# Two inner norms of a one-layer streaming encoder: the last two units before each run 384 tokens, then 256, with the norm between, and the next stage's first two units go by token halves

## The chip, the cores and the metric

One core of one Trainium2 chip runs the kernel. The metric is the device time of one execution in microseconds (us). The traces and the profile pages are of one execution each, taken by the hardware profiler; "span" is the time from the first to the last instruction in it. PE is TensorE, DVE is VectorE, ACT is ScalarE, POOL is GpSimd, SP issues the weight loads.

## The reference

One step of a hybrid encoder layer over 640 tokens: 512 of a prompt (batch 1) and 8 x 16 of samples, width 1024. Everything is fp32 in and out.

```
x += 0.5 * gate1 * SwiGLU_1(mod1(rms(x)))            # D_FF = 2816
x += gate2 * (mixer(mod2(rms(x))) @ w_out)           # w_in: 1024 -> 3664; sparse attention | gated delta net
x += 0.5 * gate3 * SwiGLU_2(mod3(rms(x)))
y  = rms(x)                                          # final norm
rms(z)  = z * rsqrt(mean(z*z over the 1024 features) + 1e-6) * gain
mod_i(z) = z * (1 + scale_i(c)) + shift_i(c)         # c: one row for the prompt, one per sample
```

"Inner norms" are the second and the third `rms`: between the first feed-forward stage and the mixer's `w_in` projection, and between the mixer's `w_out` projection and the second feed-forward stage. A norm over the features needs the sum of squares of a token over all of x, so it can't be finished for a token before the last feature tile of the stage ahead has been added for that token.

## The kernel before, in words

x is held transposed, `x_t[128, 8, 640]`: feature tile m (0 to 7) on the partitions, tokens along the row. A *unit* is one output tile of 128 features by 640 tokens. It is summed in one of two PSUM pairs (two banks, one per 320 tokens, `HALF`). A product is done in three passes so that it keeps fp32 precision: every operand is split into a rounded part (`_hi`, fp32r, made by ACT) and the remainder (`_lo`, made by DVE by a subtraction), and PE does hi x hi, hi x lo and lo x hi. So a unit over k input tiles is k x 3 x 2 matmuls of 320 columns: 36 in the last chunk of the first feed-forward stage (k = 6), 48 in the projections (k = 8). Weights are split the same way, some units ahead: `split_hi` on ACT (L335), `split_lo` on DVE (L344), in the feed-forward stages `part_hi` and `part_lo`; four slots hold split weights, and a slot is free when its unit is done.

The order of work is written out by hand for each engine; semaphores count what is done. Each engine runs its own list in order.

The stage ahead of a norm ends with eight units, one for each feature tile m of x. After each, `add_to_x` (L540) on DVE adds gate * result into `x_t`, `act_square` (L364) squares the new tile on ACT, and `pool_square_sums` (L405) on POOL adds the squares of tiles 0 to 6 into `std`. Then, at the norm:

- `sum_squares` (L3310) on PE sums over the partitions with one-column matmuls against ones: 5 token tiles of `std`, then 5 of the last square. Each fp32 matmul shows as two pieces.
- `act_std` (L376), `norm_rstd` (L389): root on ACT and reciprocal on DVE, for a column of 5 token tiles. Between the last add and the reciprocal DVE makes the tables `amp` and `gate` (L485, L506) in the first norm.
- PE (L3328) spreads the reciprocals over all partitions: 5 matmuls of 128 columns into banks 2 and 3.
- For each feature tile m: `rstd_times` (L394) on DVE multiplies x by the spread row (from PSUM), ACT scales and shifts the 512 prompt tokens, POOL does so for the 128 sample tokens in two instructions, ACT rounds (`h_hi` or `b_hi`), DVE subtracts (`h_lo` or `b_lo`). The buffers `t1` and `h32` are double. These are `act_modulate`, `dve_modulate`, `pool_modulate` (L417, L435, L459) in the first norm and the `_modulate_halves` three in the second. Only tile 0 goes in two token halves, so that the next stage can begin sooner.
- The next stage's first two units run together, one input tile at a time as it becomes ready: `project_two` (L3415) for `w_in`, `both_units` for the second feed-forward stage. For each input tile this is 12 matmuls of 320 columns.

The third unit of a next stage needs the PSUM pair of the first, so it waits until ACT has evacuated that (L1715 after the first norm, the SiLU of L1022 after the second). In the second norm ACT loads the SiLU table after its last rounding, and the fourth unit's weights are split in the midst of the norm's work (`EARLY[3]`).

The final norm is not touched. There the last four units already run for 384 tokens (`SPLIT`) and then 256.

Of the kernel before, what the change touches and what calls it, by code (L numbers as in the profile page):

```python
# [24 lines left out]
P = 128  # L25
# [178 lines left out]
def encoder_step(nc, a):  # L204

    ctx = ExitStack()
    with ctx:
# [156 lines left out]
        def act_square(act, n, x_base, m):  # L364

            if m >= 2:
                act.wait_ge(sq_summed, 6 * (n - 1) + max(m - 2, 1))
            at = 0
            if m == KD - 1:
                act.wait_ge(r_tok, 4 * n - 1)  # L370
                act.activation(sq_of[n][:, m % 2, 0:SEQ], x_t[:, m, 0:SEQ], ACT.Square).then_inc(std_done, 1)
                at = SEQ
            act.wait_ge(x_done, x_base + m + 1)
            act.activation(sq_of[n][:, m % 2, at:TOK], x_t[:, m, at:TOK], ACT.Square).then_inc(sq_done, 1)

        def act_std(act, n):  # L376

            act.wait_ge(ss_done, KD + 2 * n)
            act.activation(ss_tok[:, 1], bank[2][:, 0:NT], ACT.Sqrt, scale=1.0 / D, bias=EPS).then_inc(std_done, 1)

        def first_half(act, n, m, out, t_ap, hi):

            act.wait_ge(r_tok, 4 * n + 1)
            act.activation(out, t_ap, ACT.Identity, scale=amp[:, n, m, 0:1],
                           bias=mod[:, 3 * n * KD + m, 0:1]).then_inc(std_done, 1)
            act.wait_ge(std_done, 4 * n + 1)
            act.activation(hi, out, ACT.Copy).then_inc(std_done, 1)

        def norm_rstd(dve, n):  # L389

            dve.wait_ge(std_done, 4 * n)
            dve.reciprocal(ss_tok[:, 0], ss_tok[:, 1]).then_inc(r_tok, 1)

        def rstd_times(dve, n, out, m, halves=False):  # L394

            if halves:
                dve.wait_ge(rstd_done, 2 * n - 1)
                dve.tensor_tensor(out[:, 0:HALF], x_t[:, m, 0:HALF], bank[2][:, P:P + HALF], ALU.mult).then_inc(r_tok, 1)
                dve.wait_ge(rstd_done, 2 * n)
            at = HALF if halves else 0  # L400
            for cols, src in ((slice(at, 3 * P), bank[2][:, P + at:]), (slice(3 * P, TOK), bank[3][:, 0:2 * P])):
                ins = dve.tensor_tensor(out[:, cols], x_t[:, m, cols], src, ALU.mult)
            ins.then_inc(t_done, 1)

        def pool_square_sums(pool, n):  # L405

            for m in range(1, KD - 1):
# [5 lines left out]
                else:  # L413
                    pool.wait_ge(sq_summed, 6 * (n - 1) + m - 1)
                    pool.tensor_tensor(std_of[n], std_of[n], sq_of[n][:, m % 2], ALU.add).then_inc(sq_summed, 1)

        def act_modulate(act):  # L417
            n = 1
            act.wait_ge(tables_done, tables_at(n) + 2)
            for m in range(KD):  # L420
                g = n * KD + m
                if m == 0:
                    first_half(act, n, m, h32[:, g % 2, 0:HALF], t1[:, g % 2, 0:HALF], h_hi[:, m, 0:HALF])
                at = 0 if m else HALF
                act.wait_ge(t_done, g + 1)
                if m >= 2:
                    act.wait_ge(h_lo_done, T_LO + g - 1)
                    act.wait_ge(h_hi_done, T_HI + g - 1)
                act.activation(h32[:, g % 2, at:SEQ], t1[:, g % 2, at:SEQ], ACT.Identity,
                               scale=amp[:, n, m, 0:1], bias=mod[:, 3 * n * KD + m, 0:1]).then_inc(hp_done, 1)  # L430
                act.wait_ge(hp_done, g + 1)
                act.wait_ge(hs_done, g + 1)
                act.activation(h_hi[:, m, at:TOK], h32[:, g % 2, at:TOK], ACT.Copy).then_inc(h_hi_done, 1)
# [3048 lines left out]
```

## Time and profile before

| | us |
|---|---|
| runs (3), median | 1461.63 (1461.09 to 1462.32) |
| the profiled execution | 1461.94 |
| its span | 1460.2 |
| PE busy | 1408.6 (96%) |
| DVE busy | 897.9 (61%) |
| ACT busy | 566.6 (39%) |
| POOL busy | 387.4 (27%) |

An engine's busy time is the union of its instructions. Matmul ends are modelled, and a matmul's bar (0.31 us for 320 columns) is longer than the distance to the next one; the distance between starts is the rate. An idle engine costs nothing unless the chain that sets the end runs through it.

### The profile page before, as it was taken

To read this page: it belongs to the slowest core of one execution; us is meant where nothing else is said; L and a number is where in the kernel's file an instruction comes from. 1 tells how busy PE (TensorE), PEld (TensorE's weight loads), DVE (VectorE), ACT (ScalarE), POOL (GpSimd) and SP (SyncE) were. 2 spreads that over 40 slices of the span, in tenths; PEclk is the share of its full clock that TensorE was granted. 3 is DMA by queue.
4 is the path that set the end of the run, shared out by engine and by line. 5 is a ranking of instruction groups with operands and counts; after the bars stand their busy time and mean duration, and the time that the engine had idled before them with its cause. 6 is when DMAs were issued, how large, how long until landed. Compare 5 with 4: busy or idle time off the path is not lost. (4 is left out here: it accounts for less than half of the span.)

```text
span 1460.2 us, 28968 instructions
## 1 busy us (share of the span) xinstructions
PE 1408.6 (96%) x11663; PEld 1321.2 (90%) x11667; DVE 897.9 (61%) x1661; ACT 566.6 (39%) x1125; POOL 387.4 (27%) x352
## 2 busy tenths in 40 slices
PE   5999999999999999999999999898999999999997
PEld 5999999999999989989896677798999999999997
DVE  5546774675577452667578885745457358744864
ACT  5422431332234352654325435534433134413444
POOL 1603322340232241441002221023531134203400
PEclk9999999999999999999999999998999999999999
DMA  9534444455453324222106031241224123331231
GB/s 344 167 127 134 148 158 128 145 166 167 130 173 92 86 60 104 73 64 67 44 8 162 2 93 52 74 130 44 58 58 128 46 58 88 102 101 45 75 99 73
DMA packets 207658, 148.79 MB, mean 102 GB/s; under 512 B 21163, under 2 KB 191436, under 8 KB 207528
## 3 DMA queue, kind: packets, MB, share of 16 engines
q1 hardware_dynamic: 204360, 137.54, 31.6%
q0 software_dynamic: 3168, 9.42, 2.3%
q8 instruction: 93, 1.52, 0.5%
q14 instruction: 37, 0.30, 0.1%
HBM read 139.99 MB, written 6.95 MB: 101 GB/s over the span
## 5 line engine op out<-in xcount | busy, mean ns | idle before, releaser
L1163 PE MATMUL pair<-b_hi,w_hi 128*128 128x320 f32 x720 | 224.3, 311 | 0.0
L1163 PE MATMUL pair<-b_hi,w_lo 128*128 128x320 f32 x720 | 222.5, 309 | 0.0
L1163 PE MATMUL pair<-b_lo,w_hi 128*128 128x320 f32 x720 | 222.4, 309 | 0.0
L1276 PE MATMUL pair<-act_hi,w_hi 128*128 128x320 f32 x656 | 150.7, 311 | 0.0
L1276 PE MATMUL pair<-act_lo,w_hi 128*128 128x320 f32 x656 | 149.5, 309 | 0.0
L1276 PE MATMUL pair<-act_hi,w_lo 128*128 128x320 f32 x656 | 149.4, 309 | 0.0
L548 DVE SCALAR_TENSOR_TENSOR x_t<-pair,gate,x_t 128x320 f32<-128x320 f32 x120 | 52.5, 479 | 154.9 <-PE pair L1276 129.6
L1163 PEld LDWEIGHTS pair<-b_hi,w_hi 128*128 128x128 f32 x720 | 135.1, 188 | 7.0 <-issue 4.5
L660 ACT ACTIVATE w_hi<-sums_a 128x512 fp32r<-128x512 f32 x72 | 45.1, 626 | 246.3 <-POOL sums_a L694 129.4
L1044 DVE TENSOR_TENSOR uvw<-pair,uvw 128x320 f32<-128x320 f32 (+1 forms) x126 | 67.6, 536 | 115.6 <-PE pair L1163 115.5
L1163 PEld LDWEIGHTS pair<-b_lo,w_hi 128*128 128x128 f32 x720 | 135.2, 188 | 0.0
L1163 PEld LDWEIGHTS pair<-b_hi,w_lo 128*128 128x128 f32 x720 | 135.2, 188 | 0.0
L3394 PE MATMUL pair<-h_hi,w_hi 128*128 128x320 f32 x496 | 115.6, 314 | 1.8 <-DVEq L560 1.2
L3394 PE MATMUL pair<-h_hi,w_lo 128*128 128x320 f32 x496 | 113.0, 309 | 0.0
L3394 PE MATMUL pair<-h_lo,w_hi 128*128 128x320 f32 x496 | 112.9, 309 | 0.0
L1276 PEld LDWEIGHTS pair<-act_hi,w_hi 128*128 128x128 f32 x656 | 109.2, 188 | 3.3 <-issue 2.1
L1276 PEld LDWEIGHTS pair<-act_hi,w_lo 128*128 128x128 f32 x656 | 109.7, 188 | 0.0
L1276 PEld LDWEIGHTS pair<-act_lo,w_hi 128*128 128x128 f32 x656 | 109.7, 188 | 0.0
L666 DVE TENSOR_TENSOR w_lo<-w_raw,w_hi 128x512 fp32r<-128x512 f32 (+2 forms) x90 | 89.6, 995 | 10.9 <-ACT w_hi L660 6.5
L660 ACT ACTIVATE w_hi<-w_raw 128x512 fp32r<-128x512 f32 (+2 forms) x90 | 66.1, 737 | 76.7 <-PE pair L1276 51.3
L660 ACT ACTIVATE w_hi<-raw_more 128x512 fp32r<-128x512 f32 (+2 forms) x90 | 65.7, 736 | 71.6 <-PE pair L1276 56.1
L3394 PEld LDWEIGHTS pair<-h_hi,w_hi 128*128 128x128 f32 x496 | 82.0, 188 | 10.7 <-issue 9.2
(480 smaller groups left out, 3227.5 us busy)
## 6 DMA issues: line engine op xcount, KB each, us to landing
w_mod_raw<-w_mod SPq DMA_DIRECT2D x28, 1024.0 KB, 5.9
w_raw<-ffn_w_gate SPq DMA_DIRECT2D x40, 512.0 KB, 4.0
raw_more<-ffn_w_up SPq DMA_DIRECT2D x40, 512.0 KB, 3.8
w_raw<-w_in SPq DMA_DIRECT2D x22, 512.0 KB, 3.8
w_raw<-ffn_w_down SPq DMA_DIRECT2D x16, 384.0 KB, 3.7
raw_more<-ffn_w_down SPq DMA_DIRECT2D x16, 384.0 KB, 3.5
w_mod_a<-w_mod SPq DMA_DIRECT2D x4, 1024.0 KB, 10.7
w_mod_b<-w_mod SPq DMA_DIRECT2D x4, 1024.0 KB, 11.5
```

The lines of the kernel that those rows point to most:

```text
L548: ins = dve.scalar_tensor_tensor(out=xs, in0=src, scalar=g, in1=xs, op0=ALU.mult, op1=ALU.add)
L660: act.activation(place_of(w_hi_half, w_hi, item), stationary(item), ACT.Copy).then_inc(hi_done, item[4])
L666: dve.tensor_tensor(place_of(w_lo_half, w_lo, item), stationary(item), hi, ALU.subtract).then_inc(lo_done, item[4])
L1044: dve.tensor_tensor(out, bank_ap, other, ALU.add).then_inc(combined, 1)
L1163: mm = pe.matmul(job_bank(j, BANK_OF[part]), w[:, at, kk], mv[:, kk, s], start=(kk == 0 and v == 0 and part in FIRST_OF_BANK), stop=(kk == ...
L1276: mm = pe.matmul(pair[part % 2][:, b, 0:HALF], w[:, slot, k], mv[:, k, b * HALF:(b + 1) * HALF], start=(k == 0 and v == 0), stop=(k == n - ...
L3394: mm = pe.matmul(pair[u % 2][0:width, b, 0:HALF], w[:, 0:width], x_parts[part][:, k, b * HALF:(b + 1) * HALF], start=(k == 0 and v == 0), ...
```

## The change

1. *The last two units ahead of each norm* (tiles 6 and 7 of x). Both first run for tokens 0 to 383 (`SPLIT`), one behind the other, then both for tokens 384 to 639. `add_first_tiles` and `add_last_tiles` add the two parts to x.
2. *The norm in two parts.* Token tiles 0 to 2 and 3 to 4 each have their own sums, root, reciprocal and spread rows (`part_sums`, `root`, `inverse`, `part_rows`). The first part's sums and rows stand inside PE's passes over tokens 384 to 639; the second part's stand inside the next stage's first pass, behind its third and fifth input tile. POOL sums the squares of tiles 0 to 5 only; PE takes three sources (`std` and both squares).
3. *The next stage's first two units* go by token halves: all eight input tiles for tokens 0 to 319, then all eight for tokens 320 to 639. The multiply, scale, round and subtract of each tile are done in the same two passes. POOL's part (tokens 512 to 639) is all in the second pass.
4. *Weight splits moved.* The third `w_in` unit's split goes from the end of the first feed-forward stage into the second pass of the first norm's work; in the second norm `EARLY[2]` goes into the second pass and `EARLY[3]` behind it.
5. The tables `amp` and `gate` are made behind the adds of the first 384 tokens. Counts of semaphores are changed to fit.

The core of the diff (waits that only count differently, and the second norm's twins of what is shown, are left out):

```diff
+        def add_first_tiles(dve, n, p, m, ready):
+            dve.wait_ge(ss_done, ready)
+            dve.scalar_tensor_tensor(out=x_t[:, m, 0:SPLIT], in0=pair[p][:, 0, 0:SPLIT], scalar=gate[:, n, m, 0:1],
+                                     in1=x_t[:, m, 0:SPLIT], op0=ALU.mult, op1=ALU.add).then_inc(r_tok, 1)
...
+        def first_scaled(dve, out, m):
+            dve.tensor_tensor(out[:, 0:HALF], x_t[:, m, 0:HALF], bank[2][:, P:P + HALF], ALU.mult).then_inc(t_done, 1)
+
+        def rest_scaled(dve, out, m):
+            dve.tensor_tensor(out[:, HALF:SPLIT], x_t[:, m, HALF:SPLIT], bank[2][:, P + HALF:P + SPLIT], ALU.mult)
+            dve.tensor_tensor(out[:, SPLIT:TOK], x_t[:, m, SPLIT:TOK], bank[3][:, 0:TOK - SPLIT], ALU.mult).then_inc(t_done, 1)
...
         def act_modulate(act):
+            for m in (KD - 2, KD - 1):
+                act.wait_ge(sq_summed, m - 2)
+                act.wait_ge(r_tok, 2 + m - (KD - 2) + 1)
+                act.activation(sq_of[n][:, m % 2, 0:SPLIT], x_t[:, m, 0:SPLIT], ACT.Square).then_inc(std_done, 1)
+            root(act, 0, KD + 3)
             act.wait_ge(tables_done, tables_at(n) + 2)
+            first_of(0)
+            square_rest(KD - 2)
+            first_of(1)
+            first_of(2)
+            square_rest(KD - 1)
+            first_of(3)
+            first_of(4)
+            root(act, 1, KD + 4)
+            for m in range(5, KD):
+                first_of(m)
             for m in range(KD):
+                rest_of(m)
+                if m == 3:
+                    split_hi(act, U_IN + 2)
...
         def dve_modulate(dve):
+            for m in (KD - 2, KD - 1):
+                add_first_tiles(dve, 0, m % 2, m, KD + m - (KD - 2) + 1)
+            for k in range(1, 3):
+                dve_amp(dve, k)
+                dve_gate(dve, k)
+            inverse(dve, 0, 5)
+            first_times(0)
+            first_times(1)
+            last_tiles(KD - 2)
+            first_lo(0)
+            first_times(2)
+            first_lo(1)
+            last_tiles(KD - 1)
+            for m in range(3, KD):
+                first_times(m)
+                first_lo(m - 1)
+                if m == 5:
+                    inverse(dve, 1, 6)
+            rest_times(0)
+            first_lo(KD - 1)
+            for m in range(1, KD):
+                rest_times(m)
+                rest_lo(m - 1)
+                if m == 5:
+                    split_lo(dve, U_IN + 2)
+            rest_lo(KD - 1)
...
+            def last_two():
+                us = (U_FFN2 - 2, U_FFN2 - 1)
+                for u in us:
+                    start_unit(u)
+                    for k in range(KD):
+                        for v, (w, part) in enumerate(three_passes(u, k)):
+                            mm = pe.matmul(pair[u % 2][:, 0, 0:SPLIT], w, (h_hi, h_lo)[part][:, k, 0:SPLIT],
+                                           start=(k == 0 and v == 0), stop=(k == KD - 1 and v == 2))
                     mm.then_inc(ss_done, 1)
+                for n_, u in enumerate(us):
+                    for k in range(KD):
+                        if n_ == 0 and k == 5:
+                            part_sums(2, 0)
+                        if n_ == 1 and k == 1:
+                            part_rows(2, 0)
+                        for v, (w, part) in enumerate(three_passes(u, k)):
+                            mm = pe.matmul(pair[u % 2][:, 1, 0:TOK - SPLIT], w, (h_hi, h_lo)[part][:, k, SPLIT:TOK],
+                                           start=(k == 0 and v == 0), stop=(k == KD - 1 and v == 2))
...
+            def project_two(u, x_parts):
...
                 for b in range(2):
+                    for k in range(KD):
+                        pe.wait_ge(h_lo_done, T_LO + KD + KD * b + k + 1)
+                        for uu in (u, u + 1):
+                            for v, (w, part) in enumerate(three_passes(uu, k)):
                                 mm = pe.matmul(pair[uu % 2][:, b, 0:HALF], w, x_parts[part][:, k, b * HALF:(b + 1) * HALF],
+                                               start=(k == 0 and v == 0), stop=(k == KD - 1 and v == 2))
+                        if b == 0 and k == 2:
+                            part_sums(1, 1)
+                        if b == 0 and k == 4:
+                            part_rows(1, 1)
```

## Rows read from the trace of the kernel before

**Rows 1.** The page: busy us and share of the span; one DMA issue (last number: us to landing).
```profile
PE 1408.6 (96%) x11663; PEld 1321.2 (90%) x11667; DVE 897.9 (61%) x1661; ACT 566.6 (39%) x1125; POOL 387.4 (27%) x352
w_raw<-w_in SPq DMA_DIRECT2D x22, 512.0 KB, 3.8
```

**Rows 2.** Windows: stretch, its us, busy us by engine (starts), granted clock, DMA.
```profile
500.00:520.00 20.00, 16.61 (x104) 16.28 (x103) 12.61 (x32) 10.91 (x18) 6.67 (x11) 0.83 0.23 54
514.00:518.00 4.00, 3.97 (x15) 4.00 (x16) 3.10 (x6) 3.08 (x5) 2.41 (x6) 0.50 0.01 2
800.00:820.00 20.00, 16.77 (x304) 12.61 (x302) 16.84 (x50) 10.46 (x28) 0.00 (x0) 1.00 0.01 3
```

**Rows 3.** Timeline, first norm: start, duration, engine, line, operation [idle before <- releaser].
```profile
496.25 0.46 PE L1276 MATMUL pair<-act_hi,w_hi 128*128 128x320 f32 x2
...
508.66 1.28 PE L3322 MATMUL bank<-const,sq 128*128 128x1 f32 x10 [0.68 <-ACT sq L371]
510.50 1.38 PE L3328 MATMUL bank<-const,ss_tok 128*128 128x128 f32 x10 [0.56 <-DVE ss_tok L392]
511.57 0.49 DVE L398 TENSOR_TENSOR t<-x_t,bank 128x320 f32<-128x320 f32 x1 [1.12 <-PE bank L3328]
...
512.15 0.65 ACT L384 ACTIVATE h<-t,mod,amp 128x320 f32<-128x320 f32 x1 [2.00 <-DVE t L398]
512.83 0.47 ACT L387 ACTIVATE h_hi<-h 128x320 fp32r<-128x320 f32 x1
...
514.00 0.29 PEld L3423 LDWEIGHTS pair<-h_hi,w_hi 128*128 128x128 f32 x1 [2.31 <-issue]
```

**Rows 4.** Timeline, first norm: one loop of two steps over 640 tokens.
```profile
518.94 0.87 DVE L402 TENSOR_TENSOR t<-x_t,bank 128x384 f32<-128x384 f32 x2
...
519.73 0.81 DVE L447 TENSOR_TENSOR h_lo<-h,h_hi 128x640 fp32r<-128x640 f32 x1
...
519.89 0.92 POOL L473 TENSOR_TENSOR ts<-t,amp 128x128 f32<-128x128 f32 x1 [1.56 <-DVE t L402]
...
520.89 0.41 POOL L479 TENSOR_TENSOR h<-ts,mod 128x128 f32<-128x128 f32 x1
521.39 0.74 ACT L433 ACTIVATE h_hi<-h 128x640 fp32r<-128x640 f32 x1 [0.72 <-POOL h L479]
...
522.91 0.87 DVE L402 TENSOR_TENSOR t<-x_t,bank 128x384 f32<-128x384 f32 x2
```

**Rows 5.** Timeline: end of the first norm's work, start of the third unit.
```profile
527.60 0.83 DVE L447 TENSOR_TENSOR h_lo<-h,h_hi 128x640 fp32r<-128x640 f32 x1 [0.65 <-ACT h_hi L433]
528.46 1.06 ACT L342 ACTIVATE w_hi<-w_raw 128x1024 fp32r<-128x1024 f32 x1 [0.89 <-DVE h_lo L447]
...
529.95 0.70 ACT L1715 ACTIVATE aq_t<-pair 128x640 f32<-128x640 f32 x1 [0.42 <-PE pair L3430]
...
530.91 0.53 PE L3394 MATMUL pair<-h_hi,w_hi 128*128 128x320 f32 x2
```

**Rows 6.** Timeline, second norm: seventh unit, first multiply, last ones, third unit.
```profile
986.24 0.46 PE L3394 MATMUL pair<-h_hi,w_hi 128*128 128x320 f32 x2
...
1005.63 0.49 DVE L398 TENSOR_TENSOR t<-x_t,bank 128x320 f32<-128x320 f32 x1 [1.74 <-PE bank L3328]
...
1023.50 1.28 ACT L362 ACT_TABLE_LOAD   x1
1023.52 0.90 DVE L864 TENSOR_TENSOR b_lo<-b_raw,b_hi 128x640 fp32r<-128x640 f32 x1 [0.51 <-ACT b_hi L846]
...
1026.95 0.54 PE L1193 MATMUL pair<-b_hi,w_hi 128*128 128x320 f32 x2
```

**Rows 7.** Groups by form, 495:531: count, busy us, mean ns, idle before.
```profile
L429 ACT ACTIVATE h<-t,mod,amp 128x192 f32<-128x192 f32 x1 | 0.5, 531 | 0.0
L555 DVE TENSOR_TENSOR ts<-pair,gate 128x128 f32<-128x128 f32 x3 | 0.8, 280 | 0.0
L415 POOL TENSOR_TENSOR std<-std,sq 128x640 f32<-128x640 f32 x3 | 5.8, 1923 | 10.3 <-ACT sq L374 10.3
```

More of the change, by code:

```diff
@@ L381, in first_half @@
[L381 to L403, printed above, removed]
+                act.wait_ge(sq_summed, (KD - 3) * (n - 1) + max(m - 2, 1))
@@ new lines, in encoder_step, with root, inverse @@
+        TILES = slice(0, 3), slice(3, NT)
+        def root(act, part, ready):
+            act.wait_ge(ss_done, ready)
+            src = bank[3][:, 2 * P + 3:2 * P + NT] if part else bank[2][:, 0:3]
+            act.activation(ss_tok[:, 1, TILES[part]], src, ACT.Sqrt, scale=1.0 / D, bias=EPS).then_inc(std_done, 1)
+        def inverse(dve, part, ready):
+            dve.wait_ge(std_done, ready)
+            dve.reciprocal(ss_tok[:, 0, TILES[part]], ss_tok[:, 1, TILES[part]]).then_inc(r_tok, 1)
@@ L1031, in act_halves @@
                     if kind == "down" and j == len(chunks) - 1:
-                        if first and part >= KD - AHEAD:
+                        if first and KD - AHEAD <= part < KD - 1:
                             split_hi(act, U_IN + part - (KD - AHEAD))
@@ L1035, in act_halves @@
                             load_table(act, 3, ACT.Sqrt)
-                        if part >= 1:
+                        if part >= 1 and not (first and part == KD - 1):
                             after(part - 1)
@@ L1257, in pe_halves @@
                         mods_after(n_)
+                        continue
+                    if first and j == len(chunks) - 1 and part >= KD - 2:
                         continue
@@ L1776, in mix_act @@
             delta_act(act, *attention_act(act))
-            for u in range(U_OUT, U_FFN2):
+            for u in range(U_OUT, U_FFN2 - 1):
                 if u + AHEAD < U_FFN2:
@@ L2221, in mix_dve @@
             dve.wait_ge(S["st_out"], 16)
-            for m in range(KD):
+            for m in range(KD - 1):
                 if U_OUT + m + AHEAD < U_FFN2:
@@ L2642, in mix_pe @@
             project_mixed(last_turn)
-            for m in range(2, KD):
+            for m in range(2, KD - 2):
                 project(U_OUT + m, 0, (h_hi, h_lo))
+            last_two()
         def delta_pe(pe, begin_job, turn, values, sample_rows_turned):
@@ L3266, in _ @@
             ffn1.dve(dve, mod_place)
-            for n in range(1, 3):
-                dve_amp(dve, n)
-                dve_gate(dve, n)
             dve_modulate(dve)
@@ new lines, in part_sums @@
+            def part_sums(n, part):
+                tiles = (range(3), range(3, NT))[part]
+                pe.wait_ge(sq_summed, n * (KD - 3))
+                if n == 1 and part == 0:
+                    pe.wait_ge(std_done, 4)
+                else:
+                    pe.wait_ge(sq_done, 2 * KD if n == 1 else 3 * KD + 2 * part)
+                for n_, src in enumerate((std_of[n], sq_of[n][:, 0], sq_of[n][:, 1])):
+                    for tt in tiles:
+                        dst = bank[3][:, 2 * P + tt:2 * P + tt + 1] if part else bank[2][:, tt:tt + 1]
+                        mm = pe.matmul(dst, src[:, tt * P:(tt + 1) * P], ones[:, 0:1], start=(n_ == 0 and tt == tiles[0]),
+                                       stop=(n_ == 2), skip_group_check=True)
+                mm.then_inc(ss_done, 1)
```

385 lines of the change are left out of this document (232 added, 153 removed).

## The prediction, on record before the change was built

> **What bounds the kernel now.** I read the page first, then the 20 us windows, then the timeline around both inner norms. TensorE is busy for 1408.6 us of 1460.2 [rows 1], so only what it loses can be won. It loses most around the two norms: busy 16.61 us of 20 in 500:520, at a mean granted clock of 0.83 [rows 2]. In the timeline [rows 3] the reader is to see the serial chain of the first norm: squares, one-column sums on PE (ten matmul pieces in 1.28 us), square root, reciprocal, rows spread over the partitions (510.50), first multiply on VectorE (511.57), scaling and rounding on ScalarE (0.65 and 0.47 us), and only at 514.00 a weight load of the next stage. That stage then runs at half clock: 15 matmuls begin in 514:518, 0.267 us each [rows 2]; at full clock the unit of 496.25 to 506.81 takes 72 matmuls in 10.56 us, 0.147 each [rows 3].
>
> A common origin makes before and after comparable: T is the moment at which both last units have their first 384 tokens done. 384 of 640 columns are 0.6 of the work. First norm: both units begin at 496.25 and need 10.56 us, so T = 496.25 + 6.34 = 502.6. Second norm: they begin at 986.24 and need 96 x 0.1467 = 14.08 us, so T = 986.24 + 8.45 = 994.7 [rows 3, 6]. The third unit of the next stage starts at 530.91, T + 28.3 [rows 5], and at 1026.95, T + 32.3 [rows 6]. These two distances are what the change alters. The PE floor inside them is the other 0.4 of the old units (4.2 and 5.6 us), 14.1 us for the next two units, and the sums.
>
> **Part 1: the earlier sums.** Splitting 640 into 384 + 256 keeps the columns; I cost it at nothing. PE adds sums: three sources instead of two, 15 tiles in two pieces each are 30 pieces against 20, 10 x 0.12 = 1.2 us more per norm. The first three tiles take 18 x 0.117 = 2.1 us, placed behind 12 matmuls of the 256-pass (0.117 each, by columns: 1.4 us; 15 and 1.8 us in the second norm). The add of 384 tokens and its square hide there: before, the last unit's end (506.81) to the sums of its square (508.66) is 1.85 us with 512 columns; with 384 in one add instead of two I take 1.25, ready before 1.4. GpSimd's last sum of squares (1.92 us, [rows 7]) is of the unit before these two: nothing waits. After the sums root and reciprocal have 1.0 us of cover (0.56 needed). The amp and gate tables on VectorE (1.4 us, formerly beside the sums) lie under the sums too. Rows are spread at T + 4.6 (first norm: 1.4 + 2.1 + 0.7 + 0.35) and T + 5.3 (second: 1.8 + 2.1 + 1.05 + 0.35). From the spread to the first multiply the trace has 1.07 us [rows 3]: multiplies start at T + 5.65 and T + 6.35, where before they started at 511.57 = T + 9.0 and 1005.63 = T + 10.9 [rows 6]. Gains: **3.3 and 4.6 us**.
>
> **Part 2: the chain that feeds the next stage.** Before, each of eight features is one step over 640 tokens: multiply on VectorE, scale on ScalarE and GpSimd, round on ScalarE, subtract on VectorE. Rows 4 show what sets its pace, a loop over two steps (buffers are double): multiply 0.87, GpSimd multiply 0.92 (it starts inside VectorE's subtraction and ends 0.27 after it), GpSimd add 0.41, rounding 0.74, subtraction 0.83, and 0.2 us of hand-overs: 518.94 to 522.91 is 3.97 us, 1.98 a step. PE needs 12 x 0.147 = 1.76 a step, so before the two were nearly matched. From first multiply to last subtraction it took 16.9 us (511.57 to 528.43, [rows 5]).
> The change makes this 16 steps, and a step does not halve, because each instruction has a fixed part: rounding 640 columns takes 0.74, 320 takes 0.47; scaling 320 takes 0.65, 192 takes 0.53 [rows 3, 4, 7].
> First pass (tokens 0 to 319): ScalarE needs 0.65 + 0.02 + 0.47 - 0.09 of overlap = 1.06 a step (VectorE two instructions of 320 columns, 0.49 each less 0.08 of overlap: 0.82), against 0.88 on PE. Eight steps are 8.5 us. ScalarE also squares the last tiles of two features, takes a root (0.75 together), and twice waits for VectorE, whose queue now holds three 128-column instructions per last unit (0.28 each, [rows 7]) ahead of a subtraction: 1.3 us. First pass 10.5 us, starting 0.5 after the first multiply.
> Second pass (tokens 320 to 639): the loop over two steps is multiply 0.55 (0.49 for 320 columns, here in two instructions), GpSimd 0.40 + 0.41, rounding 0.47, subtraction 0.49 (as the multiply), hand-overs 0.2: 2.5 us if GpSimd is never held. It is held by 0.52 per loop now [rows 4]; with subtractions half as long I take half, 2.8, or **1.40 a step**. The ends are 1.26 (never held) and 1.52 (both GpSimd instructions held as today). Eight steps are 11.2 us.
> In both norms one weight split (1.06 us on ScalarE, [rows 5], and a subtraction of 1024 columns on VectorE) now stands in the second pass. Its price shows in the second norm of before, which has one already: 1005.63 to 1024.42 is 18.8 us [rows 6], 1.9 more than the first. For the first norm it is new, for the second it is another in the same place. I take 1.7.
> Sum from first multiply to last subtraction: 0.5 + 10.5 + 11.2 + 1.7 + 0.4 (tail) = 24.3. The same reckoning gives 17.2 for the first norm of before where the trace has 16.9, so I take 2% off: 23.8. Against 16.9 that is **+6.9**, against 18.8 **+5.0**.
>
> The Trainium skill, "GPSIMD Engine Reference", section Specifications, says that GpSimd's SBUF interface is shared with VectorE and contended by VectorE instructions with two SBUF inputs. The trace agrees (0.92 against 0.40), and by the rule taken strictly all GpSimd work of a loop is held, the 1.52 end: 2 us more in all.
>
> **Part 3: the hand-over.** First norm, before: last subtraction 528.43, split of unit 4 on ScalarE until 529.52, evacuation 529.95 (0.70), third unit 530.91: 2.5 us [rows 5]. After, the last PE step is half as long, but ScalarE does the same split and evacuation: 0.03 + 1.06 + 0.70 + 0.1 = 1.9. **-0.6**. Second norm, before: 1024.42 to 1026.95 = 2.5. After, ScalarE has, behind its last rounding (0.6 before the last subtraction), the other early split (1.05), the table load (1.28 + 0.21, [rows 6]) which before was under PE's long last step, and the SiLU (0.70, as the evacuation): 3.3 - 0.6 = 2.7. **+0.2**.
> Moved DMAs: SP's load of the fifth w_in unit waits for the third one's split, now at about T + 26; 3.8 us to land [rows 1], needed by a split after T + 32: hidden. GpSimd's 13 DMA issues for the mixer start with the last subtraction and shift as the rest does.
>
> **Sum.** First norm -3.3 + 6.9 - 0.6 = +3.0; second -4.6 + 5.0 + 0.2 = +0.6. Together **+3.6 us**. Half-clock matmuls (18 per norm, 0.12 each) disappear, but this is no further gain: PE then waits for the chain. Of the profiled execution (1461.94 us, 1460.2 in the span) this makes 1465.5; it stands 0.3 above the median of 1461.63, so the median after is **1465.3**.
>
> **Rivals.** *PE keeps the pace (faster).* Sixteen steps per norm, mean 1.23 us in my sum. If first and second pass overlap better than my chain has it, or instructions are shorter, each 0.11 us off the mean over 32 steps is 3.6 us: below 1.12 the change wins. At a mean of 0.97 it gives -4.7, some 1457; at PE's 0.88 all is won, about 1450. For it: the gap of 7 us is really closed, VectorE is busy only 12.6 of 20 us in 500:520. Against: ScalarE's 1.06 and the 2.5 us loop are sums of measured rows.
> *GpSimd is never held (no change).* 16 x 0.14 = 2.2 less: 1463.1.
> *The clock stays low (slower).* After the norm PE works in bursts of 0.88 with 0.2 to 0.5 us of waiting. At half clock a burst is 6 x 0.267 = 1.6 us, above both passes, and 16 of them give T + 35.5 and T + 36.3 instead of 31.3 and 32.9: +11.2 in all, 1473; a part of it 1467 or more. Against: in 800:820 PE is busy 16.77 of 20 with many short waits and clock 1.00 [rows 2]; at 514 it was low after sparse one-column work and three waits [rows 3]. The Trainium skill, "TensorE: Matmul & The Clock Gate", section HAM oscillation, warns that bursts with waits between can keep the clock falling; no row of before shows it at this duty.
> *It does not do what it says.* GpSimd's sum or the root comes late and PE stands inside the 256-pass; at most 2 us per norm, 1466 to 1468.
>
> **Chances.** What can be told from no change is 0.2%, 2.9 us: 1458.7 to 1464.5. Forecast (chain-bound, own range 1463.5 to 1468) 0.49, of which 0.37 lies above 1464.5; never held 0.17, same; PE keeps the pace 0.22, of which 0.18 faster; clock 0.08 and late sums 0.04, slower mostly. Faster 0.18, same 0.34, slower 0.48. Range 1458 to 1469: it leaves out the lower half of the fast rival and most of the clock one.
>
> **What would show it.** Multiplies at T + 5.7 and T + 6.4; no PE wait above 1 us between the stages; clock 1.00 in both; first-pass subtractions 1.06 to 1.1 apart, second-pass 1.4 apart, GpSimd multiplies of 0.4 and of 0.6 to 0.7 mixed; PE waiting 0.2 to 0.5 before each step for the subtraction; the third units at T + 31.3 and T + 32.9. Wrong if second-pass steps come 1.1 apart or less, if PE's clock is 0.50 in the passes, or if a later stage takes up the delay.

## The result, and the profile after

| | before | after |
|---|---|---|
| median of 6 runs each, same chip | 1461.32 us | 1467.18 us (1466.08 to 1469.87) |
| ratio | 1 | 1.0044, 95% interval 1.0033 to 1.0055 |
| profiled execution (span) | 1461.94 (1460.2) | 1469.87 (1468.1) |
| third unit, first norm | T + 28.3 | T + 31.9 |
| third unit, second norm | T + 32.3 | T + 35.4 |

The change makes the kernel 5.9 us slower by the medians, where 3.6 was forecast. The profiled execution was the slowest of its six. Of its 7.9 us of added span, 3.6 lie between T and the third unit in the first norm and 3.1 in the second. The other 1.2 lie outside: 0.5 ahead of the first T, 0.6 between the norms, where in 920:940 the granted clock was 0.91 in this execution and 1.00 before.

The page of after, its first row, then the windows around the two norms (columns as in [rows 2]):

```profile
PE 1415.3 (96%) x11687; PEld 1323.7 (90%) x11687; DVE 902.2 (61%) x1688; ACT 574.9 (39%) x1154; POOL 382.1 (26%) x350
```

```profile
500.00:520.00 20.00, 18.36 (x133) 17.49 (x132) 11.39 (x33) 11.25 (x24) 1.22 (x1) 1.00 0.10 27
520.00:540.00 20.00, 15.81 (x94) 13.51 (x93) 13.86 (x36) 11.98 (x22) 14.17 (x27) 1.00 0.28 63
...
1000.00:1020.00 20.00, 19.09 (x125) 18.56 (x124) 10.00 (x29) 10.54 (x22) 0.53 (x1) 0.83 0.00 1
1020.00:1040.00 20.00, 16.18 (x93) 14.53 (x92) 13.14 (x26) 13.63 (x23) 15.44 (x23) 0.91 0.23 66
```

PE's hole of 500:520 (16.61 busy at clock 0.83, [rows 2]) is filled, and a new one stands in 520:540: 15.81 busy. The work was moved, the loss moved behind it. The timeline of the first norm shows the earlier start (T is the first 256-column matmul, 503.08):

```profile
503.08 0.28 PE L1449 MATMUL pair<-act_hi,w_hi 128*128 128x256 f32 x1
...
504.66 0.80 PE L3489 MATMUL bank<-const,std 128*128 128x1 f32 x6
...
507.81 0.83 PE L3498 MATMUL bank<-const,ss_tok 128*128 128x128 f32 x6
...
508.68 0.89 DVE L407 TENSOR_TENSOR t<-x_t,bank 128x320 f32<-128x320 f32 x2 [1.39 <-PE bank L3498]
```

The first multiply comes at T + 5.6, where it came at T + 9.0 [rows 3]. Then the second pass, one turn of the loop over two steps, which answers to [rows 4]:

```profile
523.14 0.49 DVE L491 TENSOR_TENSOR h_lo<-h,h_hi 128x320 fp32r<-128x320 f32 x1 [0.40 <-ACT h_hi L440]
...
523.55 0.21 DVE L411 TENSOR_TENSOR t<-x_t,bank 128x64 f32<-128x64 f32 x1
523.68 0.41 DVE L412 TENSOR_TENSOR t<-x_t,bank 128x256 f32<-128x256 f32 x1
...
524.17 0.41 POOL L543 TENSOR_TENSOR ts<-t,amp 128x128 f32<-128x128 f32 x1 [0.28 <-DVE t L412]
...
524.66 0.59 POOL L549 TENSOR_TENSOR h<-ts,mod 128x128 f32<-128x128 f32 x1
...
525.34 0.47 ACT L440 ACTIVATE h_hi<-h 128x320 fp32r<-128x320 f32 x1 [0.30 <-POOL h L549]
...
525.85 0.49 DVE L491 TENSOR_TENSOR h_lo<-h,h_hi 128x320 fp32r<-128x320 f32 x1 [0.40 <-ACT h_hi L440]
```

523.14 to 525.85 is 2.71 us for two steps, 1.36 a step: a chain in which every engine waits for the one ahead. VectorE's multiply of 523.55 had its inputs long before, and its buffer had been read by 522.19, by ScalarE's scaling two steps back; it stood in VectorE's queue behind the subtraction of 523.14, which waited for ScalarE. The end of the pass, with the split on VectorE in it, and the hand-over, as in [rows 5]:

```profile
528.15 1.22 DVE L347 TENSOR_TENSOR w_lo<-w_raw,w_hi 128x1024 fp32r<-128x1024 f32 x1
...
530.29 0.42 PE L3620 MATMUL pair<-h_hi,w_hi 128*128 128x320 f32 x1 [0.86 <-DVE h_lo L491]
...
532.53 0.49 DVE L491 TENSOR_TENSOR h_lo<-h,h_hi 128x320 fp32r<-128x320 f32 x1 [0.35 <-ACT h_hi L440]
...
534.97 0.53 PE L3586 MATMUL pair<-h_hi,w_hi 128*128 128x320 f32 x2 [0.72 <-ACTq L1890]
```

The second norm is the same with one thing more: the clock fell three times, first behind the one-column sums (1004.3 to 1007.7), then in the first pass, at the one-column sums of the second part (1014.5 to 1018.0), and last at 1031.6, under the last steps. Its rows and the end of the first pass, then two steps of the second pass, then the hand-over:

```profile
1001.75 1.48 PE L3489 MATMUL bank<-const,sq 128*128 128x1 f32 x12
...
1004.85 1.48 PE L3498 MATMUL bank<-const,ss_tok 128*128 128x128 f32 x6
...
1006.37 0.88 DVE L407 TENSOR_TENSOR t<-x_t,bank 128x320 f32<-128x320 f32 x2 [2.72 <-PE bank L3498]
...
1008.17 0.47 ACT L931 ACTIVATE b_hi<-b_raw 128x320 fp32r<-128x320 f32 x1 [0.55 <-PE pair L3518]
...
1012.88 0.31 PE L1335 MATMUL pair<-b_hi,w_lo 128*128 128x320 f32 x1
...
1015.31 0.47 PE L1335 MATMUL pair<-b_lo,w_hi 128*128 128x320 f32 x1
...
1018.12 0.61 PE L3498 MATMUL bank<-const,ss_tok 128*128 128x128 f32 x4
...
1018.76 0.22 DVE L411 TENSOR_TENSOR t<-x_t,bank 128x64 f32<-128x64 f32 x1 [0.90 <-PE bank L3498]
...
1019.23 0.49 DVE L977 TENSOR_TENSOR b_lo<-b_raw,b_hi 128x320 fp32r<-128x320 f32 x1
```

```profile
1022.21 0.59 POOL L1033 TENSOR_TENSOR ts<-t,amp 128x128 f32<-128x128 f32 x1 [0.89 <-DVE t L412]
...
1023.24 0.41 POOL L1033 TENSOR_TENSOR ts<-t,amp 128x128 f32<-128x128 f32 x1
```

```profile
1031.57 0.73 DVE L990 TENSOR_TENSOR b_lo<-b_raw,b_hi 128x320 fp32r<-128x320 f32 x1 [0.35 <-ACT b_hi L941]
...
1032.50 1.28 ACT L362 ACT_TABLE_LOAD   x1
...
1033.90 0.69 ACT L1161 ACTIVATE silu<-pair 128x640 f32<-128x640 f32 x1
...
1034.78 0.64 PE L1335 MATMUL pair<-b_hi,w_hi 128*128 128x320 f32 x2 [0.21 <-ACTq L1164]
```

The six pieces that spread the rows take 1.48 us, where the same six took 0.83 in the first norm: the lower of the clock's two levels, 1.2 GHz and not 2.4. So the slow clock reaches the chain in three places: the first rows come 0.65 late, ScalarE's first rounding, whose buffer the eighth unit still reads, waits 0.55 until that unit is half through, and VectorE waits 0.90 for the second part's rows, which stand in PE's list behind matmuls at half speed (1015.31, 0.47 instead of 0.31).

In this norm's second pass the subtractions come 1.83 and 0.98 apart in turn (1022.05, 1023.88, 1024.86), 1.40 a step in the mean, and it is GpSimd's multiply that is held every second time (0.59, then 0.41); in the first norm it was its add.

### The profile page after: what moved, and what is told of

The parts are those of the page before. It is cut to its first block and busy times, and to the rows that moved or that the text cites. A ratio compares the mean times of both kernels' runs of the same rounds, so it can differ in the third digit from the quotient of the medians.

```text
span 1468.1 us, 29092 instructions
## 1 busy us (share of the span) xinstructions
PE 1415.3 (96%) x11687; PEld 1323.7 (90%) x11687; DVE 902.2 (61%) x1688; ACT 574.9 (39%) x1154; POOL 382.1 (26%) x350
## 3 DMA queue, kind: packets, MB, share of 16 engines
q1 hardware_dynamic: 204360, 137.54, 31.3%
## 5 line engine op out<-in xcount | busy, mean ns | idle before, releaser
L1425 PE MATMUL pair<-act_hi,w_hi 128*128 128x320 f32 x632 | 145.3, 311 | 0.0
L1425 PE MATMUL pair<-act_lo,w_hi 128*128 128x320 f32 x632 | 144.0, 309 | 0.0
L1425 PE MATMUL pair<-act_hi,w_lo 128*128 128x320 f32 x632 | 143.9, 309 | 0.0
L3586 PE MATMUL pair<-h_hi,w_hi 128*128 128x320 f32 x464 | 108.2, 315 | 2.4 <-DVEq L628 1.2
L1425 PEld LDWEIGHTS pair<-act_hi,w_hi 128*128 128x128 f32 x632 | 105.2, 188 | 3.3 <-issue 2.1
L3586 PE MATMUL pair<-h_hi,w_lo 128*128 128x320 f32 x464 | 105.7, 309 | 0.0
L1425 PEld LDWEIGHTS pair<-act_hi,w_lo 128*128 128x128 f32 x632 | 105.7, 188 | 0.0
L1425 PEld LDWEIGHTS pair<-act_lo,w_hi 128*128 128x128 f32 x632 | 105.6, 188 | 0.0
L3586 PE MATMUL pair<-h_lo,w_hi 128*128 128x320 f32 x464 | 105.6, 309 | 0.0
L1305 PE MATMUL bank<-b_hi,w_hi 128*128 128x320 f32 x288 | 89.2, 310 | 0.0
```

The costliest lines, as they stand in the source:

```text
L1305: mm = pe.matmul(job_bank(j, BANK_OF[part]), w[:, at, kk], mv[:, kk, s], start=(kk == 0 and v == 0 and part in FIRST_OF_BANK), stop=(kk == ...
L1425: mm = pe.matmul(pair[part % 2][:, b, 0:HALF], w[:, slot, k], mv[:, k, b * HALF:(b + 1) * HALF], start=(k == 0 and v == 0), stop=(k == n - ...
L3586: mm = pe.matmul(pair[u % 2][0:width, b, 0:HALF], w[:, 0:width], x_parts[part][:, k, b * HALF:(b + 1) * HALF], start=(k == 0 and v == 0), ...
```

## The experiments

Each kernel's median is of 5 to 12 executions. The kernels from one row with a time in brackets to the next ran on one chip beside the kernel before, whose median there stands in the brackets; medians of different groups are best compared by their ratios. The distances from T to the third unit are of the one profiled execution of each, which need not be its median run; the clock is the mean granted clock of 500:520, 520:540, 1000:1020 and 1020:1040.

| kernel | median us (before) | ratio, 95% interval | third units, T + | clock |
|---|---|---|---|---|
| splits moved | 1463.53 (1461.22) | 1.0015 [1.0007, 1.0024] | 30.5, 31.9 | 1.00 1.00 1.00 1.00 |
| sums spread | 1465.01 | 1.0026 [1.0017, 1.0035] | 33.2, 33.7 | .91 .91 .91 .91 |
| no GpSimd | 1463.56 | 1.0015 [1.0004, 1.0027] | 31.1, 33.9 | 1.00 .91 .83 1.00 |
| four by halves | 1465.95 | 1.0032 [1.0020, 1.0044] | 31.6, 34.6 | 1.00 1.00 .91 1.00 |
| two, splits moved | 1467.86 (1460.66) | 1.0048 [1.0034, 1.0062] | 32.3, 35.0 | .87 .96 .75 1.00 |
| four, splits moved | 1462.86 | 1.0013 [1.0004, 1.0022] | 30.1, 31.3 | 1.00 1.00 1.00 1.00 |
| six, splits moved | 1463.80 | 1.0021 [1.0011, 1.0031] | 31.0, 33.7 | 1.00 1.00 .91 1.00 |
| the changed one again | 1466.39 | 1.0043 [1.0029, 1.0057] | 32.5, 34.8 | .91 1.00 .91 .91 |
| multiply ahead | 1460.17 (1461.50) | 0.9988 [0.9979, 0.9997] | 30.2, 32.6 | .91 1.00 .86 1.00 |
| four, ahead, split in pause | 1459.22 | 0.9984 [0.9976, 0.9993] | 28.8, 29.6 | .97 .94 1.00 1.00 |
| before, with multiply ahead | 1459.70 | 0.9987 [0.9978, 0.9996] | 27.9, 30.6 | .83 1.00 .74 1.00 |
| four, ahead, split behind | 1457.92 (1461.54) | 0.9977 [0.9968, 0.9986] | 30.1, 28.8 | .83 1.00 1.00 1.00 |

### The splits out of the second pass

```diff
             for m in range(KD):
                 rest_of(m)
-                if m == 3:
-                    split_hi(act, U_IN + 2)
+            split_hi(act, U_IN + 2)
...
-                if in_same_run(u):
+                if in_same_run(u) and v:
                     wait_extra(act, u + AHEAD)
                     split_hi(act, u + AHEAD)
```

(the second norm's two splits likewise: one behind the last feature, one behind the first SiLU)

> The changed kernel, with each weight split that stands inside the second pass moved behind the last feature, and the next one (first norm: the split of the fourth unit; second norm: the second early one) moved behind the evacuation or SiLU of the first unit. Theory A (the chain of ScalarE, VectorE and GpSimd sets the pace, and the splits cost 1.7 us a norm in it and up to 1 us at the hand-over): the three waits of 0.75 to 0.86 us at 528 to 532 go, the third units start at T + 29.4 to 30.2 (31.9 in the changed kernel) and T + 32.3 to 33.5 (35.2); together 3.5 to 5 us less, 1462.2 to 1463.7. Theory B (what is lost is lost to the clock of TensorE, half for three stretches of the second norm): the splits lie in slack, the third units move by under 0.5 us, 1466.5 to 1467.2.

1463.53: 3.6 us less than the changed kernel's 1467.18 (both against 1461.2 to 1461.3 before). In the first norm the three waits of 0.75 to 0.86 are gone: subtractions come 1.35 apart to the end. The splits' price, forecast at 1.7 a norm, is 1.4 there (31.9 to 30.5). In the second norm PE still waits 0.72 to 0.89 at every second step, without any split. The third unit comes 3.5 us earlier there, and here the clock stayed at 1.00 with the same instructions around the sums:

```profile
995.91 0.28 PE L3513 MATMUL pair<-h_hi,w_hi 128*128 128x256 f32 x1
...
1001.15 0.83 PE L3493 MATMUL bank<-const,ss_tok 128*128 128x128 f32 x6
...
1002.01 0.89 DVE L407 TENSOR_TENSOR t<-x_t,bank 128x320 f32<-128x320 f32 x2 [1.82 <-PE bank L3493]
...
1013.43 0.49 DVE L972 TENSOR_TENSOR b_lo<-b_raw,b_hi 128x320 fp32r<-128x320 f32 x1
...
1024.62 0.73 DVE L985 TENSOR_TENSOR b_lo<-b_raw,b_hi 128x320 fp32r<-128x320 f32 x1 [0.35 <-ACT b_hi L939]
```

First multiply at T + 6.1; in the changed kernel at T + 7.0. From there to the end of the first pass's last subtraction (1013.43 here, 1019.23 there) it takes 11.9 us and not 13.4, and on to the end of the last one 11.4 and not 12.6. The hand-over is 2.5 in both. The first multiply's 0.9 and the first pass's 1.4, together 2.3 us, lie where PE ran at half clock in the changed kernel and at full clock here; the second pass's 1.15 is the split's. That is one execution of each. Of the 3.6 us between the medians the splits' 1.4 and 1.15 are 2.6. The rest may be the clock's: the granted clock of the whole execution was 0.995 or more in 11 of 12 executions here, and in 2 of the 11 of the changed kernel (the six above and the five of its repetition below).

### The sums spread

```diff
-                            if part == KD - 2 and k == 4:
-                                part_sums(1, 0)
+                            if part == KD - 2 and k in (2, 3, 4):
+                                part_sums(1, 0, k - 2)
```

> The changed kernel, with the one-column matmuls of the token sums put one source at a time behind three successive steps where that is possible (both first sums, the second sums of the second norm) and not in one run of 18 or 12. Theory A (chain): the rows come no later than 0.5 us, nothing is won, 1466.7 to 1467.7; the granted clock of the second norm may rise without moving the third unit. Theory B (the clock falls after the runs of one-column matmuls, and this costs the second norm its 2.3 us over the forecast): the clock is 1.00 in 1000:1020 (0.83 in the changed kernel), the matmul pieces that spread the rows take 0.83 us in all again and not 1.48, the third unit of the second norm is at T + 33 and not T + 35.2; 1465.0 to 1465.5.

The clock was 0.91 in all four windows, and the rows of the second norm took 1.48 us again. So the clock can fall without a run of 18 one-column matmuls. The median, 1465.01, is nevertheless 2.2 below 1467.18, and the profiled execution (1468.32) was the slowest of its twelve, so no trace shows a typical one. The clock of the whole execution, which is on record for each, goes with the time: 0.991 for the two slowest (1468.32 and 1468.23), 0.996 and 0.997 for the three fastest (1463.53 to 1463.88), and it was 0.995 or more in 6 of 12, against 2 of 11 for the changed kernel. So spreading the sums doesn't prevent the fall; it may make it rarer, which a dozen executions of each, not on one chip, don't settle.

### Without GpSimd in the loop

```diff
-                of_tokens(m, slice(HALF, TOK), SEQ, 2 * KD + m + 1)
+                of_tokens(m, slice(HALF, TOK), TOK, 2 * KD + m + 1)
```

(and GpSimd only counts up its semaphores)

> The changed kernel, without scale and shift of the samples' own tokens on GpSimd (128 of 640 columns): ScalarE scales them with the prompt's values in its own instruction, so part of the result is left out. Theory A: the second pass goes at 1.36 us a step because GpSimd's multiply and add (0.41 and 0.59) stand in the loop; without them ScalarE sets the pace, 0.65 + 0.47 less overlap = 1.06 to 1.10 a step; 16 steps by 0.27 to 0.30 are 4.3 to 4.8 us less, 1462.4 to 1462.9. Rival: VectorE (multiplies in two instructions, subtractions, waits between) sets the pace; GpSimd only fills its slack, steps stay at 1.3 or more, 1466 to 1467.

Second pass, two subtractions in a row:

```profile
519.66 0.66 ACT L435 ACTIVATE h<-t,mod,amp 128x320 f32<-128x320 f32 x1
519.72 0.49 DVE L491 TENSOR_TENSOR h_lo<-h,h_hi 128x320 fp32r<-128x320 f32 x1
...
520.35 0.47 ACT L440 ACTIVATE h_hi<-h 128x320 fp32r<-128x320 f32 x1
...
520.85 0.49 DVE L491 TENSOR_TENSOR h_lo<-h,h_hi 128x320 fp32r<-128x320 f32 x1 [0.18 <-ACT h_hi L440]
```

1.13 a step (0.66 + 0.47) and not 1.36: GpSimd is in the loop, and without it ScalarE is the bound (its scaling and rounding follow each other without a pause). 3.6 us less, 4.3 to 4.8 expected; the two steps around the split still take 2.0 each.

### Fewer features by halves

```diff
+        H1, H2 = 4, 4
...
             def rest_of(m):
-                of_tokens(m, slice(HALF, TOK), SEQ, 2 * KD + m + 1)
+                if m < H1:
+                    of_tokens(m, slice(HALF, TOK), SEQ, KD + passed(H1, m), KD + passed(H1, m - 2))
+                else:
+                    of_tokens(m, slice(0, TOK), SEQ, KD + passed(H1, m), KD + passed(H1, m - 2), 2)
```

> The changed kernel, with only the first four features by token halves (second half's sums right behind the first feature's step, its rows behind the second's) and the last four whole, 640 tokens a step: twelve steps and not sixteen. Theory A (fixed part of each instruction): four first-pass steps of 1.06, four second-pass steps of 1.36 and four whole ones of 1.98 are 17.6 us against 19.4 for the sixteen, and PE's work on the first half is no longer all ahead of the second, so that the whole steps (1.76 us of PE each) wait little; with the earlier multiplies kept, the third units start at T + 27 to 29 and T + 30 to 32 (changed: 31.9 and 35.2; before: 28.3 and 32.3). Time 1457 to 1461, faster than before or the same. Rival: with coarse steps PE stands 0.5 us or more ahead of each again and its clock falls as it did before (0.83 in 500:520), which eats the gain: 1461 to 1464.

A miss: 1465.95, only 1.2 of the 5.9 us back, and that within the intervals. ScalarE takes the second root only behind all its first passes (512.08), and then has nothing until the second multiplies (1.93 us idle before 514.16); the split stands among whole steps and makes one of them 2.7 us long (subtractions at 522.05 and 524.72). The next three kernels have the root earlier and the splits behind, with two, four and six features by halves (with two, the root stands behind the second feature, as there is no fourth; it is the four and six that have the lines shown):

```diff
             for m in range(2, H1):
+                if m == 3:
+                    root(act, 1, KD + 4)
                 first_of(m)
-            root(act, 1, KD + 4)
```

> Only the first two features by token halves, six whole; the weight splits moved behind the norm (as in the kernel of the moved splits, third units there at T + 30.5 and T + 31.9 in the profile, 1463.5); second root as soon as its sums are there. Theory A (a sum of fixed step times, plus the moment at which the second rows are there): ten steps, but after the two first-pass steps the chain is idle until the second multiplies, which can't start before about T + 12.1; then 2 x 1.36 + 6 x 1.98 = 14.6 and 2.3 for the hand-over: T + 29.0, second norm T + 30.0 to 30.5. Together 3 to 3.5 us below 1463.5: 1460.0 to 1461.0. Rival (the wait for the second rows hurts more than the steps give, since TensorE stands still and its clock falls): third units no earlier than T + 30.5 and T + 32, 1463 or more.

> The same with four features by halves: first passes of 1.06 just fill the time up to the second multiplies (T + 12.1), then 4 x 1.36 + 4 x 1.98 = 13.4 and 2.3: T + 27.8, second norm T + 29 to 29.5. Theory A: 4.5 to 5 us below 1463.5, 1458.5 to 1459.5, faster than before by 2 us. Rival (TensorE's steps of 1.76 us and their queue, not the chain, end last; whole steps of 2.6 us as in the kernel with four features above, where a split stood among them): third units at T + 29.5 and T + 31.5, 1461 to 1462.5, no faster than before.

> The same with six features by halves. Theory A: 6 x 1.06 + 1.3 for squares and root = 7.7 us of first pass from T + 6.15, no waiting for the second rows, then 6 x 1.36 + 2 x 1.98 = 12.1 and 2.3: T + 28.3 to 28.6, second norm T + 29.5 to 30.2; 3.5 us below 1463.5, 1459.5 to 1460.5, between four and eight features. Rival (number of steps does not matter, the change costs by what it does to TensorE's clock or by the sums): 1463 as with eight.

PE at the switch to the second half, with two features, then with four:

```profile
518.83 0.60 PE L3635 MATMUL pair<-h_hi,w_hi 128*128 128x320 f32 x1 [2.94 <-DVE h_lo L506]
```

```profile
516.61 0.38 PE L3635 MATMUL pair<-h_hi,w_hi 128*128 128x320 f32 x1 [1.45 <-DVE h_lo L506]
...
523.03 0.56 PE L3635 MATMUL pair<-h_hi,w_hi 128*128 128x320 f32 x2 [1.38 <-DVE h_lo L506]
```

Four (1462.86) and six (1463.80) don't differ by more than their intervals from eight (1463.53); two is worst (1467.86), PE standing 2.94 us and running at clock 0.87 and 0.75. All three forecasts missed, by 6.9, 3.4 and 3.3 us from the nearer end. The sum of step times left out what PE loses at the two switches, from first to second pass (1.45) and from half to whole steps (1.38). I read these waits as the depth of the chain, from a multiply to its subtraction; no run tests that. The number of steps alone isn't what costs.

### The changed kernel again

> The changed kernel once more, unaltered, on the same chip as the three with two, four and six features. Theory A: 1466.5 to 1467.5; third units at T + 31.9 and, with the clock fallen to half behind the sums of the second norm as in the first profile, T + 35.2; if the clock doesn't fall there this time, T + 33.3. Rival: the second norm's 35.2 is not the clock's doing and stays at full clock too.

1466.39, ratio 1.0043: the result repeats. The clock fell in both norms now (T + 32.5, T + 34.8). In the second norm the first multiply is at T + 7.6. What the third unit's distance is at full clock this run can't say; the rows of the kernel with the splits moved do.

### The multiply two features ahead of the subtraction

The loop of the second pass reads: subtraction, multiply behind it in VectorE's queue, GpSimd, rounding, subtraction. One link is only an order of instructions:

```diff
-            for m in range(1, KD):
+            rest_times(1)
+            for m in range(2, KD):
                 rest_times(m)
-                rest_lo(m - 1)
+                rest_lo(m - 2)
+            rest_lo(KD - 2)
             rest_lo(KD - 1)
```

> The kernel of the moved splits (eight features by halves, 1463.5, third units at T + 30.5 and T + 31.9), with one edit: VectorE issues the second pass's multiply of feature m + 2 ahead of the subtraction of feature m, not behind it. Theory A, sharpened (the second pass's 1.36 us a step is a wait in VectorE's queue: the multiply of the step after next stands behind a subtraction that waits for ScalarE, and only then can GpSimd and ScalarE begin): steps fall to ScalarE's own 1.05 to 1.10, third units at T + 28.3 and T + 29.7, 1459 to 1460. Rival (GpSimd, held by VectorE's instructions, sets the pace, or the two buffers of the scaled feature, each free only after its subtraction, do): steps of 1.3 or more, 1463 as without the edit.

> Four features by halves and four whole (1462.9, third units at T + 30.1 and T + 31.3), with the same reordering on VectorE, and each norm's weight split put into the pause between the two passes, where ScalarE and VectorE wait for the second rows. Theory A: half steps 1.05 to 1.10, whole steps 1.76 to 1.85 (TensorE's own pace); the chain is 2.0 us shorter a norm, but TensorE already worked without a gap over the last four features, so 1.2 to 1.5 a norm: T + 28.7 and T + 29.8, 1460 and a little below; faster than before by no more than 1 us. Rival (the two passes cost TensorE its waits at the start and the switch, 0.7 + 1.4 + 0.7 + 1.4, whatever VectorE's order): T + 30 and T + 31, 1462.5.

> The kernel before the change, with the same reordering alone: VectorE multiplies feature m + 2 ahead of the subtraction of feature m, in both norms. Theory A: its 1.98 us a step fall to about TensorE's 1.76 at full clock, eight steps by 0.2 are 1.6 us a norm, but its first matmuls run at half clock (0.267 us, 3.2 a step), which the clock and not the chain sets there; 1.0 to 2.5 us less in all, 1458.5 to 1460. If so, the change's shorter steps would have to be measured against this kernel. Rival (as before the step is bound by the buffers and GpSimd): 1460.5 to 1461.5, the same.

With eight by halves: 1460.17, 3.4 less, with steps of 1.15 us in the first norm (519.36 to 527.40 are seven) and not 1.36; in the second mostly 1.09. The expected 1.05 to 1.10 fails in the first norm by 0.05 or more, where GpSimd's instructions are held more often (0.65). The kernel is now faster than before the change, though the clock was half around its first rows (0.91 and 0.86), and the third units came 1.9 and 2.9 us later than expected in that execution. With four by halves 1459.22. And the old kernel with the same order has steps of 1.53 where it had 1.98:

```profile
517.53 0.82 DVE L449 TENSOR_TENSOR h_lo<-h,h_hi 128x640 fp32r<-128x640 f32 x1
518.27 0.88 DVE L402 TENSOR_TENSOR t<-x_t,bank 128x384 f32<-128x384 f32 x2
519.07 0.82 DVE L449 TENSOR_TENSOR h_lo<-h,h_hi 128x640 fp32r<-128x640 f32 x1
```

1459.70: PE's 1.76 is then the longer, and its half clock at the start (0.83 and 0.74, as before) sets the rest. In the first norm the old loop had not held PE at all: between 514.03 and 530.91 it shows no wait of 0.2 us, and the third unit comes only 0.4 earlier with the new order (T + 27.9 for 28.3). The gain is in the second norm (T + 30.6 for 32.3), where PE had waited 0.62 and 0.30 and now doesn't. So with the order mended, the change as made (with its splits moved) is worth nothing, 1460.17 against 1459.70.

In the kernel with four by halves the split in the pause made PE wait 2.31 us at the switch. Last, the split behind again:

```diff
-            split_hi(act, U_IN + 2)
             for m in range(KD):
                 rest_of(m)
+            split_hi(act, U_IN + 2)
```

> Four features by halves, VectorE's multiplies two ahead of its subtractions, and the weight splits not in the pause between the passes (there TensorE waited 2.31 and 2.27 us for the first subtraction of the second pass, against 1.45 and 1.40 without a split) but behind the last feature again. Theory A (from the second pass on TensorE works without a gap, so all that is left to win lies ahead of it, and a split behind the last feature is hidden under TensorE's last steps, which end 2 us after the chain): the waits at the switch fall back to 1.45 and 1.40, third units at T + 27.9 and T + 28.8 against 28.75 and 29.6; 1.7 us less, 1457.5. Rival (the splits at the end are seen again at the hand-over, 1.0 us and more a norm): 1459.2 as before or above.

```profile
1010.50 0.39 PE L1355 MATMUL pair<-b_hi,w_hi 128*128 128x320 f32 x1 [1.41 <-DVE b_lo L1010]
...
1020.08 1.28 ACT L362 ACT_TABLE_LOAD   x1
...
1023.12 0.53 PE L1355 MATMUL pair<-b_hi,w_hi 128*128 128x320 f32 x2
```

1457.92, ratio 0.9977 [0.9968, 0.9986]: the lowest of all, 3.6 us below the kernel before. The second norm is where it was expected (T + 28.8), with the table load ended 1.8 us ahead of the third unit; in the first norm the clock fell again (T + 30.1, expected 27.9). The intervals overlap with those of the same kernel with the split in the pause (0.9984) and of the old kernel with the new order alone (0.9987), and the chips differ: that four features by halves add anything to the new order is likely by the second norm's trace, and not shown by the times.

## Why the prediction was right, and where it was short

The forecast (chain-bound, slower, 1465.3) held in sign and mechanism; 1467.18 lies within the likeliest case's own range (1463.5 to 1468), 1.9 above the forecast. The added time is 5.9 us for 3.6: the sign and the loop were right, the size is 2.3 us short, mostly by the clock in the second norm (below). Step by step:

- *Earlier sums.* Multiplies forecast at T + 5.65 and 6.35: 5.6, and 6.1 at full clock. Right; in the changed kernel's own second norm 7.0 and 7.6, because PE was at half clock ahead of the rows.
- *First pass.* 11.0 us from the first multiply to ScalarE's last rounding of the pass: 11.5 (508.68 to 520.21). The subtractions were to come 1.06 to 1.1 apart; of the seven distances three are 1.05 to 1.15, the others, where ScalarE squares, takes the root or waits, 1.39 to 1.89. ScalarE's wait of 0.55 for PE's sums of the second part, ahead of the root, stood in no term.
- *Second pass.* 1.40 a step: 1.36 in the first norm, 1.40 in the second. Right as a sum of the loop's links. In the second norm it is also right in the instruction held, GpSimd's multiply of 0.59 and 0.41 in turn; in the first its add is held (0.59) and the multiply isn't (0.41 except at the split). The Trainium skill, "SBUF — State Buffer", section "SBUF: two separate sides", calls the port that GpSimd and VectorE share an exclusive lock for whole instructions; the trace agrees in that both sides stretch: 0.49 becomes 0.71 for a subtraction of VectorE that starts inside a GpSimd instruction in the kernel with the multiply ahead (524.00). It stretches by 0.22, though, with 0.36 of GpSimd's instruction still to come, so a wait for the whole of it doesn't show in these rows.
- *What I didn't ask:* whether the loop had to be one. I summed multiply, GpSimd, rounding and subtraction as given and took "PE keeps the pace" to be a matter of overlapping passes or shorter instructions. A changed order in one queue was worth 3.4 us, nearly the whole forecast loss.
- *The splits.* 1.7 in a norm; 1.4 measured in the first, 1.15 in the second.
- *The chain in all, first norm.* 24.3 by the terms, 23.8 after the 2% taken off: 24.3 (508.68 to 533.02). The 2% were no gain, and that the terms add up is in part luck: the first pass is 0.5 too short and the second with its split 0.6 too long.
- *Hand-over.* 1.9 and 2.7: 1.95 (533.02 to 534.97) and 2.5 (1032.30 to 1034.78).
- *First norm in all.* T + 31.3 forecast, 31.9 measured, +3.6 for +3.0.
- *Second norm: the mis-sized term.* +0.6 forecast, +3.1 measured in the first profile and +2.5 in the second. The step "clock 1.00 in both" failed. It was 0.83 and 0.91 (profile one), 0.91 and 0.91 (two); T + 35.4 is 0.65 late at the first multiply and 2.1 in the chain from there to the last subtraction, nearly all of it in the first pass, where PE's matmuls ran at half speed from 1014.9 to 1018.0. With clock 1.00 and the splits moved the same stage ended at T + 31.9; with the split's 1.15 added that is T + 33.1, against 32.9 forecast. So the sum holds at full clock, and the clock's price in this norm is 2.3 us in the first profile. Of the rival "the clock stays low", given 0.08, a part came true, by another way than it says: the clock fell behind the one-column sums, in both profiles, and in the first profile also in the bursts of the first pass; what it delayed was the rows and one rounding. In the second pass's bursts it was 1.00 until 1031.6.
- *Earlier sums and root in time:* yes, no PE wait in the 256-column passes. "No PE wait above 1 us between the stages": 0.70.

## What to carry to other kernels

When a chain over several engines is slower a step than its busiest engine (here 1.36 against ScalarE's 1.06, 1.98 against PE's 1.76), look for an instruction that stands ready in a queue behind one that waits. Moving it costs nothing, and here it gained 3.4 us in the new kernel and 1.8 in the old, where the rebuilt norm by itself lost 2.3 even with its splits moved. It pays only where PE waits for the chain, which in the old kernel's first norm it did not. Splitting steps to start earlier pays only while the halves are shorter by as much: each instruction keeps its fixed part, and each switch, to the second half or to another step size, cost PE about 1.4 us here. And a stage whose clock may fall has two prices; give both.

## What the runs showed of the hardware

The granted clock fell to half in the midst of back-to-back matmuls of 256 columns, at the tenth behind the run of 18 one-column ones (1001.17 to 1003.10), with no wait of PE above 0.2 us ahead of it. The timeline of after, second norm, between 0.12 and 0.21 us from start to start:

```profile
1004.01 0.28 PE L3518 MATMUL pair<-h_lo,w_hi 128*128 128x256 f32 x1
1004.13 0.28 PE L3518 MATMUL pair<-h_hi,w_lo 128*128 128x256 f32 x1
1004.25 0.37 PE L3518 MATMUL pair<-h_hi,w_hi 128*128 128x256 f32 x1
1004.42 0.42 PE L3518 MATMUL pair<-h_lo,w_hi 128*128 128x256 f32 x1
1004.63 0.42 PE L3518 MATMUL pair<-h_hi,w_lo 128*128 128x256 f32 x1
```

The same instructions ran at 1.00 in another kernel's execution. Spreading the one-column matmuls over three steps didn't prevent it. The time of one kernel's executions goes with it: for the changed one, 1469.87 us at a granted clock of 0.991 over the whole execution, 1466.08 at 0.995. The third units of its two profiles differ by 0.6. What decides whether it falls, these runs don't show.
